# Last block of a three-block model: order of the compression block, of a weight slot's rounding, and of the second branch's gating

## The chip, the core and the metric

One NeuronCore of a Trainium2 chip runs the whole program. The metric is the device time of one execution in microseconds, from its start to its end; the median of several runs counts. Engines are named PE (TensorE), ACT (ScalarE), DVE (VectorE), POOL (GpSimd) and SP (SyncE, which only issues loads and stores here).

## What is computed

Three residual blocks on a sequence of 256 tokens of width 1024, all in float32: two of a first kind, each with a feed-forward part, and a last one, `second_block`, which the change touches. Cut to what matters:

```python
def second_block(x, ...):
    h = rms_norm_2(x, norm_w)
    proj = h @ w_in          # q_a k_a v_a z_a q_b kc vc ksl vsl kwn vwn gate_b z_b gate_m
    o_a = moba_mixer(norm(q_a), norm(k_a), v_a, bias_a)              # 8 heads
    k_cmp = norm(compress(kc, pos_k, w1_k, w2_k))                    # gelu(windows @ w1) @ w2
    v_cmp = compress(vc, pos_v, w1_v, w2_v)
    o_b = nsa_mixer(norm(q_b), k_cmp, v_cmp, norm(ksl), vsl, norm(kwn), vwn, gate_b, bias_b)
    y_a = o_a * silu(z_a)
    y_b = o_b * silu(z_b)
    g_m = sigmoid(gate_m)
    merged = g_m[:, :1024] * (y_a @ w_branch_a) + g_m[:, 1024:] * (y_b @ w_branch_b)
    return x + merged @ w_out
```

## The kernel before

**Weights.** Every weight matrix is cut into slots of at most 128 x 2048 numbers, listed in the order of use (L263 to L284). SP loads slot n into one of four buffers `raw`; the buffer of slot n-4 must be free (L491). For a product in near float32 accuracy, ACT rounds the slot into `whi` (two halves, L1217 and L1218, in `high`), and POOL writes `wlo = raw - whi` (L531, four instructions a slot). There are three buffers of each, so the rounding of a slot waits until the one three before it is used. PE then does three matmuls for each piece (L545 to L547): high by high, low by high, high by low. The activations are kept transposed and split the same way: `T_hi` (ACT, L1249) and `T_lo` (DVE, L1755) make `Th` and `Tl` from what PE has transposed into PSUM (`to_T`, L635). A raw buffer is free when its low half is done. The four slots of the compression's first matrices (`whole`: k0, k1, v0, v1) are used raw, without rounding, by `cmp_hidden` (L1076), and free their buffer when PE has used them.

**Order.** Each engine has one instruction queue, written out by hand. In the last block all four share one scheme, `pairs` (PE at L816, ACT at L1441, DVE at L1946): twelve pairs of attention heads, each with scores on PE (L847), score plus bias on DVE (L1954), exponential on ACT (L1447), a transposition on PE (`turn`), its copy on ACT (`turned`, L1457 and L1458), values on PE (L836) and the write on DVE (`finish`). Into each pair, at the places "x", "a", "m" and "b", other work is hung by a table `keyed`. PE fills the pairs with the weight slots (`slot_tm`): za, ksv and zb in pairs 1 to 3, the gates GA and GB in pairs 4 to 10, YA in pair 11 and in the tail; YB, the merge and the output matrix "fo" come after.

**Around the change.** In pair 1, PE does za0, then `cmp_hidden(0, 0)`, which waits for both windows (DVE, L2204, keys first, then values), since the keys' hidden layer goes to bank 1, where the projection that both windows read lies. In pair 3, ACT does squares and copies of "ksv" (L1636, L1640), its root, the exponentials, and after them rounds zb1. At the end, DVE gates the second branch (L2328) in one go when all pairs are written; `turn_b` (PE, L1140) transposes it ahead of the last k step of slot YA1, and YB0 uses it.

Of the kernel before, what the change touches and what calls it, by code (L numbers as in the profile page):

```python
# [16 lines left out]
ALU = mybir.AluOpType  # L17
# [5 lines left out]
P = 128  # L23
S = 256
NT = S // P
# [122 lines left out]
def build(nc, I, out, known):  # L148
    ctx = ExitStack()
    with ctx:  # L150
# [120 lines left out]
        for part in (lambda: za(0), lambda: hidden("k", 0), lambda: za(1), lambda: hidden("k", 1),  # L271
                     lambda: hidden("v", 0), lambda: sel(0), lambda: hidden("v", 1), lambda: sel(1)):
            part()
# [265 lines left out]
        def _(pe):  # L539
# [526 lines left out]
            def cmp_hidden(a, j):  # L1066

                if j == 0:
                    pe.wait_ge(*read(("kc", 0)))
                    pe.wait_ge(*read(("vc", 0)))  # L1070
                    pe.wait_ge(*at("gb"))
                n = slot_no[("w1" + "kv"[a], j)]
                pe.wait_ge(*at(f"w_raw{n % NRAW}", n))
                for k in range(8):
                    q = 32 * (k % 4)
                    i = mm(PS[q:q + 32, 1 - a, 0:256], XC[a][:, 8 * j + k, :], raw[n % NRAW][:, k * 256:(k + 1) * 256],  # L1076
                           start=j == 0 and k < 4, stop=j == 1 and k >= 4)
                i.then_inc(*done("w_used", n))

            def cmp_fold(a):  # L1080

                pe.wait_ge(*at("c_part", a))
                if a == 0:
                    pe.wait_ge(*read(("zb", 1)))
                for m in range(2):
                    i = mm(PS[:, 1 - a, 256 + 32 * m:256 + 32 * m + 32], part[:, a, m * P:(m + 1) * P], cc("four"),
                           start=True, stop=True)
                i.then_inc(*done("c_ht", a))

            def cmp_keys():  # L1090
                pe.wait_ge(*at("c_hid"))
                pe.wait_ge(*at("load_w2"))
                for m in range(2):
                    i = mm(PS[0:32, 1, 0:DH], hid[:, m, :], w2c[:, 0, m, :], start=m == 0, stop=m == 1)
                i.then_inc(*done("c_k"))
# [44 lines left out]
            def turn_b():  # L1140
                pe.wait_ge(*at("y2b"))
                to_T("y2b", hn[:, :, 512:D], 4, 4)
# [5 lines left out]
            def branch_a1(last_values):  # L1148
                pe.wait_ge(*read((("GB", 1), 1)))
                slot_tm((("YA", 1), 0), 2, 8, True, True, mids={1: last_values, 3: turn_b})  # L1150
# [10 lines left out]
            def gate_z(nm, hf):  # L1161
                if (nm, hf) == ("za", 0):
                    pe.wait_ge(*at("hT", (2, 1)))
                if (nm, hf) == ("zb", 0):
# [8 lines left out]
                     for w in range(2) for h in range(NH)], True,  # L1173
                  keyed({(0, "a"): (keys_in,), (0, "m"): (gates_T,), (0, "b"): (lambda: head_T("qb", 2, 2),),
                         (1, "a"): (lambda: gate_z("za", 0), lambda: cmp_hidden(0, 0)),
# [12 lines left out]
            slot_tm((("YB", 0), 0), 6, 12, True, True, fresh="y2b", f0=0)  # L1188
# [13 lines left out]
        def _(act):  # L1202
# [464 lines left out]
            def cmp_part(a):  # L1667
                act.wait_ge(*at("w_used", slot_no[("w1" + "kv"[a], 1)]))
                act.activation(part[:, a, :], PS[:, 1 - a, 0:256], ACT.Copy).then_inc(*done("c_part", a))

            def cmp_gelu(a):
                act.wait_ge(*at("c_ht", a))
                h = PS[:, 1 - a, 256:320].rearrange("p (m c) -> p m c", m=2)
                if a == 0:
                    act.activation(hid[:, :, :], h, ACT.Gelu_apprx_tanh).then_inc(*done("c_hid"))
                    return
                for m in range(2):
                    i = act.activation(hidr[:, m, :].rearrange("p (g h c) -> p g h c", g=2, h=4),
                                       bc(h[:, m, :].rearrange("p (g c) -> p g c", g=2), 2, 4), ACT.Gelu_apprx_tanh)
                i.then_inc(*done("c_rep"))  # L1680
# [31 lines left out]
            def next_tb(h):  # L1712
# [5 lines left out]
                (1, "b"): (lambda: high(slot_no[("ksv", 0)]), lambda: z_tanh("za", za, 2)),  # L1718
                (2, "a"): (lambda: next_tb(0), lambda: cmp_part(0), lambda: high(slot_no[("ksv", 1)])),
                (2, "b"): (lambda: cmp_part(1), lambda: high(slot_no[("zb", 0)]), lambda: head_squares("ksv", 2)),  # L1720
                (3, "x"): (lambda: head_root("ksv"),),
                (3, "a"): (lambda: next_tb(4), lambda: high(slot_no[("zb", 1)])),
                (3, "b"): (lambda: head_T("ksv", 3, kswT, (qn + 3, qn + 4), 2), lambda: high(slot_no[(("GA", 0), 0)]),
                           lambda: z_tanh("zb", zb, 0)),
                (4, "a"): (lambda: high(slot_no[(("GA", 0), 1)]),),
# [9 lines left out]
            T_hi("y2b", 4, 12, 4, lambda k: None)  # L1735
            after_slot((("YA", 1), 0))
            after_slot((("YB", 0), 0))
# [7 lines left out]
        def _(dve):  # L1745
# [525 lines left out]

            def sigmoid(nm, n, t):

                g = sg[(nm, n)]
                dve.wait_ge(*read(((nm, n), t)))
                lk(ts(g[:, t, :], g[:, t, :], 0.5, 0.5, ALU.mult, ALU.add))
# [19 lines left out]
            def att_write(p, rc, o):  # L2296
# [26 lines left out]
                (10, "a"): (lambda: T_lo("y2a", 4, 8, 0, lambda k: None),),  # L2323
                (11, "a"): (lambda: sigmoid("GB", 1, 0), lambda: sigmoid("GB", 1, 1))}))
            dve.wait_ge(*at("a_o", ("att", 11)))
            dve.wait_ge(*read(("zb", 1)))
            for t in range(NT):
                i = stt3(out=hn[:, t, 512:D], in0=hn[:, t, 512:D], scalar=0.5, in1=zb[:, t, :], op0=ALU.mult, op1=ALU.mult)  # L2328
            i.then_inc(*done("y2b"))
            T_lo("y2b", 4, 12, 4, lambda k: None)  # L2330
# [51 lines left out]
```

## Time and profile before

| | |
|---|---|
| median of three runs | 1010.84 us (1009.25 to 1011.47) |
| the profiled execution | 1008.57 us |
| its span | 1006.7 us |
| PE busy | 966.7 us, 96% |
| POOL busy | 676.6 us, 67% |
| ACT busy | 605.5 us, 60% |
| DVE busy | 471.2 us, 47% |
| granted clock of PE, mean | 0.992 |
| memory read | 175.47 MB, 180 GB/s |

The span is the time between the first and the last instruction; what lies around it is 1.9 us. The attention part of the last block goes from about 814 to 968 us of the span, and the tail to 1006.7. All times in the text are those of the span. In a timeline, a line with [t <-who] says that the engine stood still for t before it, and what ended that.

### The profile page before, as it was taken

How to read it: one execution, taken by the hardware profiler on the slowest of the kernel's cores; microseconds unless marked ns; L12 is line 12 of the kernel's file. 1: busy time of each engine (PE TensorE's matmuls, PEld its weight loads, DVE VectorE, ACT ScalarE, POOL GpSimd, SP SyncE). 2: the span in 40 equal slices, each digit the busy share in tenths (PEclk: the TensorE clock that was granted, in tenths of full speed). 3: DMA queues.
4: the chain of work that ended last, by engine and by line, in shares of the span. 5: the costliest groups of instructions: out<-in, count | busy, mean ns of one | idle time of the engine just before them, and what ended most of it. 6: DMA issues, size and time to landing. Idle time of an engine off the chain costs nothing. (4 is left out here: it accounts for less than half of the span.)

```text
span 1006.7 us, 15876 instructions
## 1 busy us (share of the span) xinstructions
PE 966.7 (96%) x6093; PEld 847.1 (84%) x6093; DVE 471.2 (47%) x990; ACT 605.5 (60%) x1130; POOL 676.6 (67%) x538
## 2 busy tenths in 40 slices
PE   6999998999999999999999899999999999899998
PEld 5888788999999797888877799999987887688777
DVE  4735334453434645776944544444346131233552
ACT  7636656555555676877967664555557464685531
POOL 5977725766666785797778575757777855485664
PEclk9999999999999999999998999999999999999999
DMA  9684424776554556457456356565555537544221
GB/s 334 224 236 150 157 84 147 233 240 196 189 188 168 175 143 201 143 161 245 165 178 219 130 186 210 167 209 168 175 175 199 178 120 269 192 127 166 85 84 42
DMA packets 124952, 177.64 MB, mean 176 GB/s; under 512 B 13185, under 2 KB 86797, under 8 KB 124685
## 3 DMA queue, kind: packets, MB, share of 16 engines
q1 hardware_dynamic: 120701, 168.91, 51.7%
q10 hardware_dynamic: 4176, 7.71, 2.2%
q8 instruction: 48, 0.79, 0.3%
q14 instruction: 27, 0.22, 0.1%
HBM read 175.47 MB, written 5.24 MB: 180 GB/s over the span
## 5 line engine op out<-in xcount | busy, mean ns | idle before, releaser
L531 POOL TENSOR_TENSOR wlo<-raw,whi 128x512 fp32r<-128x512 f32 (+1 forms) x502 | 656.4, 1342 | 301.0 <-ACT whi L1217 285.1
L548 PE MATMUL PS<-Th,whi 128*128 128x256 f32 (+2 forms) x1000 | 285.8, 286 | 3.5 <-DVE Tl L1755 2.8
L549 PE MATMUL PS<-Tl,whi 128*128 128x256 f32 (+2 forms) x1000 | 282.5, 283 | 0.0
L550 PE MATMUL PS<-Th,wlo 128*128 128x256 f32 (+2 forms) x1000 | 282.4, 283 | 0.0
L1217 ACT ACTIVATE whi<-raw 128x1024 fp32r<-128x1024 f32 (+1 forms) x144 | 150.7, 1047 | 161.6 <-PE PS L550 122.5
L1830 DVE SCALAR_TENSOR_TENSOR arena<-PS,cols,arena 128x255 f32<-128x255 f32 (+1 forms) x272 | 118.5, 477 | 192.1 <-ACT arena L1350 165.6
L545 PE MATMUL PS<-whi,Th 128*128 128x512 f32 x480 | 194.2, 405 | 9.7 <-DVE Tl L1804 3.3
L548 PEld LDWEIGHTS PS<-Th,whi 128*128 128x128 f32 (+2 forms) x1000 | 191.3, 191 | 9.9 <-issue 5.9
L549 PEld LDWEIGHTS PS<-Tl,whi 128*128 128x128 f32 (+2 forms) x1000 | 191.4, 191 | 1.7 <-issue 0.7
L550 PEld LDWEIGHTS PS<-Th,wlo 128*128 128x128 f32 (+2 forms) x1000 | 191.2, 191 | 0.1
L547 PE MATMUL PS<-whi,Tl 128*128 128x512 f32 x480 | 188.9, 393 | 0.0
L546 PE MATMUL PS<-wlo,Th 128*128 128x512 f32 x480 | 188.8, 393 | 0.0
L1218 ACT ACTIVATE whi<-raw 128x1024 fp32r<-128x1024 f32 (+1 forms) x144 | 149.5, 1038 | 0.0
L545 PEld LDWEIGHTS PS<-whi,Th 128*128 128x128 f32 x480 | 91.1, 190 | 36.5 <-issue 12.4
L547 PEld LDWEIGHTS PS<-whi,Tl 128*128 128x128 f32 x480 | 91.1, 190 | 19.7
L546 PEld LDWEIGHTS PS<-wlo,Th 128*128 128x128 f32 x480 | 91.1, 190 | 17.8 <-issue 0.5
L545 PE MATMUL PS<-whi,aTh 128*128 128x512 f32 x176 | 69.0, 392 | 0.9 <-POOL wlo L531 0.9
L546 PE MATMUL PS<-wlo,aTh 128*128 128x512 f32 x176 | 68.8, 391 | 0.0
L547 PE MATMUL PS<-whi,aTl 128*128 128x512 f32 x176 | 68.5, 389 | 0.0
L1763 DVE TENSOR_TENSOR wlo<-raw,whi 128x2048 fp32r<-128x2048 f32 x18 | 41.4, 2301 | 13.4 <-ACT whi L1218 13.4
L1350 ACT ACTIVATE arena<-PS,cols 128x256 f32<-128x256 f32 x88 | 44.0, 550 | 0.0
L1359 ACT ACTIVATE aTh<-arena 128x512 fp32r<-128x512 f32 x22 | 13.9, 632 | 45.3 <-DVE arena L1849 45.3
(242 smaller groups left out, 1038.7 us busy)
## 6 DMA issues: line engine op xcount, KB each, us to landing
raw<-in_ffn_w_up_dram SPq DMA_DIRECT2D x44, 1024.0 KB, 5.1
raw<-in_w_in_dram SPq DMA_DIRECT2D x23, 1024.0 KB, 5.2
raw<-in_ffn_w_down_dram SPq DMA_DIRECT2D x22, 1024.0 KB, 4.9
raw<-in_c_w_in_dram SPq DMA_DIRECT2D x16, 1024.0 KB, 5.3
raw<-in_ab_w_in_dram SPq DMA_DIRECT2D x14, 1024.0 KB, 6.6
raw<-in_c_w_out_dram SPq DMA_DIRECT2D x8, 1024.0 KB, 5.1
raw<-in_ab_w_out_dram SPq DMA_DIRECT2D x4, 1024.0 KB, 5.8
raw<-in_c_w_in_dram SPq DMA_DIRECT2D x8, 512.0 KB, 5.3
```

The source lines that it names most:

```text
L531: i = nc.gpsimd.tensor_tensor(lo_of(n)[:, c:e], raw[n % NRAW][:, c:e], hi_of(n)[:, c:e].bitcast(F32), ALU.subtract)
L545: mm(o, ah, wh, start=first, stop=False)
L546: mm(o, ah, wl, start=False, stop=False)
L547: return mm(o, al, wh, start=False, stop=last)
L548: mm(o, wh, ah, start=first, stop=False)
L549: mm(o, wh, al, start=False, stop=False)
L550: return mm(o, wl, ah, start=False, stop=last)
L1217: act.activation(hi_of(n)[:, 0:hf], raw[n % NRAW][:, 0:hf], ACT.Copy).then_inc(*done("w_hi_half", n))
L1218: act.activation(hi_of(n)[:, hf:width], raw[n % NRAW][:, hf:width], ACT.Copy).then_inc(*done("w_hi", n))
L1350: act.activation(fac[i % 2][:, q, :], PS[:, 2 * (i % 2) + q // 2, (q % 2) * S:(q % 2 + 1) * S], ACT.Identity, scale=col(f"fw{l}1", j), bia ...
L1763: tt(lo_of(n)[:, :], raw[n % NRAW][:, :], hi_of(n)[:, :].bitcast(F32), ALU.subtract)\
L1830: return stt3(out=dst[:, a:a + n], in0=src[:, b:b + n], scalar=ws, in1=dst[:, a:a + n], op0=ALU.mult, op1=ALU.add)
```

## The change

In words: (1) the first key block of the compression stands at the head of pair 1, ahead of za0, in the list of slots and on PE; it waits for the key windows and the gate columns alone, the value block for the value windows, and the two hidden layers change banks; ACT rounds ksv0 in the middle of pair 1. (2) ACT rounds slot zb1 in pair 2, ahead of the squares of ksv, and each gate slot behind it takes the place of the one before. (3) DVE gates the second branch in two halves, one after the tenth pair's write, one after the last; PE transposes the first in YA1, the second inside YB0; `T_hi` and `T_lo` follow in two parts.

```diff
@@ -268,7 +268,7 @@
         hidden = lambda nm, j: fm("w1" + nm, I["cmp_w1_" + nm + "_2"][0], 0, k0=8 * j, j=j)
         sel = lambda hf: wide(("ksv", hf), w2, 4 * hf, KV + 256, 4, 512)
         za = lambda hf: wide(("za", hf), w2, 4 * hf, 1536, 4, 512)
-        for part in (lambda: za(0), lambda: hidden("k", 0), lambda: za(1), lambda: hidden("k", 1),
+        for part in (lambda: hidden("k", 0), lambda: za(0), lambda: za(1), lambda: hidden("k", 1),
                      lambda: hidden("v", 0), lambda: sel(0), lambda: hidden("v", 1), lambda: sel(1)):
             part()
         tm("zb", w2, KV + 792)
@@ -1066,14 +1066,13 @@
             def cmp_hidden(a, j):
 
                 if j == 0:
+                    pe.wait_ge(*(read(("vc", 0)) if a else at("gb")))
                     pe.wait_ge(*read(("kc", 0)))
-                    pe.wait_ge(*read(("vc", 0)))
-                    pe.wait_ge(*at("gb"))
                 n = slot_no[("w1" + "kv"[a], j)]
                 pe.wait_ge(*at(f"w_raw{n % NRAW}", n))
                 for k in range(8):
                     q = 32 * (k % 4)
-                    i = mm(PS[q:q + 32, 1 - a, 0:256], XC[a][:, 8 * j + k, :], raw[n % NRAW][:, k * 256:(k + 1) * 256],
+                    i = mm(PS[q:q + 32, a, 0:256], XC[a][:, 8 * j + k, :], raw[n % NRAW][:, k * 256:(k + 1) * 256],
                            start=j == 0 and k < 4, stop=j == 1 and k >= 4)
                 i.then_inc(*done("w_used", n))
 
@@ -1083,12 +1082,13 @@
                 if a == 0:
                     pe.wait_ge(*read(("zb", 1)))
                 for m in range(2):
-                    i = mm(PS[:, 1 - a, 256 + 32 * m:256 + 32 * m + 32], part[:, a, m * P:(m + 1) * P], cc("four"),
+                    i = mm(PS[:, a, 256 + 32 * m:256 + 32 * m + 32], part[:, a, m * P:(m + 1) * P], cc("four"),
                            start=True, stop=True)
                 i.then_inc(*done("c_ht", a))
 
             def cmp_keys():
                 pe.wait_ge(*at("c_hid"))
+                pe.wait_ge(*at("c_rep"))
                 pe.wait_ge(*at("load_w2"))
                 for m in range(2):
                     i = mm(PS[0:32, 1, 0:DH], hid[:, m, :], w2c[:, 0, m, :], start=m == 0, stop=m == 1)
@@ -1137,9 +1137,9 @@
                 pe.wait_ge(*at("y2a"))
                 to_T("y2a", hn, 4, 0)
 
-            def turn_b():
-                pe.wait_ge(*at("y2b"))
-                to_T("y2b", hn[:, :, 512:D], 4, 4)
+            def turn_b(k):
+                pe.wait_ge(*at("y2b", k))
+                to_T("y2b", hn[:, :, 512:D], k + 2, 4, k)
 
             def branch_a0():
                 pe.wait_ge(*at("T_lo", ("y2a", 3)))
@@ -1147,7 +1147,7 @@
 
             def branch_a1(last_values):
                 pe.wait_ge(*read((("GB", 1), 1)))
-                slot_tm((("YA", 1), 0), 2, 8, True, True, mids={1: last_values, 3: turn_b})
+                slot_tm((("YA", 1), 0), 2, 8, True, True, mids={1: last_values, 2: lambda: turn_b(0)})
 
             def keys_in():
                 pe.wait_ge(*read(("va", 1)))
@@ -1172,7 +1172,7 @@
                               lambda c, h=h, w=w: vsw[:, c, w, DH * (h // 4):DH * (h // 4) + DH])
                      for w in range(2) for h in range(NH)], True,
                   keyed({(0, "a"): (keys_in,), (0, "m"): (gates_T,), (0, "b"): (lambda: head_T("qb", 2, 2),),
-                         (1, "a"): (lambda: gate_z("za", 0), lambda: cmp_hidden(0, 0)),
+                         (1, "a"): (lambda: cmp_hidden(0, 0), lambda: gate_z("za", 0)),
                          (1, "b"): (lambda: gate_z("za", 1), lambda: cmp_hidden(0, 1)),
                          (2, "a"): (lambda: cmp_hidden(1, 0), lambda: selected(0)),
                          (2, "b"): (lambda: cmp_hidden(1, 1), lambda: selected(1)),
@@ -1185,7 +1185,8 @@
                          (7, "a"): (G("GB", 0, 0),), (7, "m"): (cmp_turn,),
                          (8, "a"): (G("GB", 0, 1),), (8, "m"): (cmp_out,),
                          (9, "a"): (G("GB", 1, 0), turn_a), (10, "a"): (G("GB", 1, 1),), (11, "a"): (branch_a0,)}), branch_a1)
-            slot_tm((("YB", 0), 0), 6, 12, True, True, fresh="y2b", f0=0)
+            pe.wait_ge(*at("a_o", ("att", 11)))
+            slot_tm((("YB", 0), 0), 6, 12, True, True, fresh="y2b", f0=0, mids={1: lambda: turn_b(2)})
 
             def turn_merged(n):
                 pe.wait_ge(*at("mrg", n))
@@ -1666,11 +1667,11 @@
 
             def cmp_part(a):
                 act.wait_ge(*at("w_used", slot_no[("w1" + "kv"[a], 1)]))
-                act.activation(part[:, a, :], PS[:, 1 - a, 0:256], ACT.Copy).then_inc(*done("c_part", a))
+                act.activation(part[:, a, :], PS[:, a, 0:256], ACT.Copy).then_inc(*done("c_part", a))
 
             def cmp_gelu(a):
                 act.wait_ge(*at("c_ht", a))
-                h = PS[:, 1 - a, 256:320].rearrange("p (m c) -> p m c", m=2)
+                h = PS[:, a, 256:320].rearrange("p (m c) -> p m c", m=2)
                 if a == 0:
                     act.activation(hid[:, :, :], h, ACT.Gelu_apprx_tanh).then_inc(*done("c_hid"))
                     return
@@ -1715,14 +1716,14 @@
 
             pairs("att", 12, True, keyed({
                 (0, "b"): (lambda: head_T("qb", 2, qbT, (qn + 7, qn + 7), 2),),
-                (1, "b"): (lambda: high(slot_no[("ksv", 0)]), lambda: z_tanh("za", za, 2)),
+                (1, "m"): (lambda: high(slot_no[("ksv", 0)]),), (1, "b"): (lambda: z_tanh("za", za, 2),),
                 (2, "a"): (lambda: next_tb(0), lambda: cmp_part(0), lambda: high(slot_no[("ksv", 1)])),
-                (2, "b"): (lambda: cmp_part(1), lambda: high(slot_no[("zb", 0)]), lambda: head_squares("ksv", 2)),
+                (2, "b"): (lambda: cmp_part(1), lambda: high(slot_no[("zb", 0)]), lambda: high(slot_no[("zb", 1)]),
+                           lambda: head_squares("ksv", 2)),
                 (3, "x"): (lambda: head_root("ksv"),),
-                (3, "a"): (lambda: next_tb(4), lambda: high(slot_no[("zb", 1)])),
-                (3, "b"): (lambda: head_T("ksv", 3, kswT, (qn + 3, qn + 4), 2), lambda: high(slot_no[(("GA", 0), 0)]),
+                (3, "a"): (lambda: next_tb(4), lambda: high(slot_no[(("GA", 0), 0)])),
+                (3, "b"): (lambda: head_T("ksv", 3, kswT, (qn + 3, qn + 4), 2), lambda: high(slot_no[(("GA", 0), 1)]),
                            lambda: z_tanh("zb", zb, 0)),
-                (4, "a"): (lambda: high(slot_no[(("GA", 0), 1)]),),
                 (4, "m"): (lambda: cmp_gelu(0), lambda: cmp_gelu(1), U((("GA", 0), 0))),
                 (4, "b"): (lambda: gates("GA", 0), cmp_norm),
                 (5, "a"): (U((("GA", 0), 1)),), (5, "m"): (U((("GA", 1), 0)),), (5, "b"): (cmp_keys,),
@@ -1732,8 +1733,9 @@
                 (9, "m"): (U((("GB", 1), 0)),), (9, "b"): (lambda: T_hi("y2a", 4, 8, 0, lambda k: None),),
                 (10, "m"): (lambda: gates("GB", 1), U((("GB", 1), 1))),
                 (11, "b"): (U((("YA", 0), 0)),)}))
-            T_hi("y2b", 4, 12, 4, lambda k: None)
+            T_hi("y2b", 2, 12, 4, lambda k: None)
             after_slot((("YA", 1), 0))
+            T_hi("y2b", 4, 12, 4, lambda k: None, 2)
             after_slot((("YB", 0), 0))
             T_hi("mrg0", 4, 0, 6, lambda k: None)
             after_slot((("YB", 1), 0))
@@ -2269,6 +2271,13 @@
                     i = stt3(out=hn[:, t, 0:512], in0=hn[:, t, 0:512], scalar=0.5, in1=za[:, t, :], op0=ALU.mult, op1=ALU.mult)
                 i.then_inc(*done("y2a"))
 
+            def gated_b(k):
+                dve.wait_ge(*at("a_o", ("att", 9 + k)))
+                dve.wait_ge(*read(("zb", 1)))
+                a = 512 + k * P
+                stt3(out=hn[:, :, a:a + 2 * P], in0=hn[:, :, a:a + 2 * P], scalar=0.5, in1=zb[:, :, k * P:(k + 2) * P],
+                     op0=ALU.mult, op1=ALU.mult).then_inc(*done("y2b", k))
+
             def sigmoid(nm, n, t):
 
                 g = sg[(nm, n)]
@@ -2320,14 +2329,12 @@
                 (7, "a"): (cmp_probs, lambda: sigmoid("GA", 1, 0), lambda: sigmoid("GA", 1, 1)),
                 (8, "b"): (cmp_out, cmp_add),
                 (9, "a"): (lambda: sigmoid("GB", 0, 0), lambda: sigmoid("GB", 0, 1)),
-                (10, "a"): (lambda: T_lo("y2a", 4, 8, 0, lambda k: None),),
+                (10, "a"): (lambda: T_lo("y2a", 4, 8, 0, lambda k: None),), (10, "b"): (lambda: gated_b(0),),
                 (11, "a"): (lambda: sigmoid("GB", 1, 0), lambda: sigmoid("GB", 1, 1))}))
             dve.wait_ge(*at("a_o", ("att", 11)))
-            dve.wait_ge(*read(("zb", 1)))
-            for t in range(NT):
-                i = stt3(out=hn[:, t, 512:D], in0=hn[:, t, 512:D], scalar=0.5, in1=zb[:, t, :], op0=ALU.mult, op1=ALU.mult)
-            i.then_inc(*done("y2b"))
-            T_lo("y2b", 4, 12, 4, lambda k: None)
+            gated_b(2)
+            T_lo("y2b", 2, 12, 4, lambda k: None)
+            T_lo("y2b", 4, 12, 4, lambda k: None, 2)
             branch_a(0)
             branch_a(1)
             for n in range(2):
```

## Rows read from the trace of the kernel before

**Rows 1.** The page's busy times: engine, busy us, share of the span, instructions.

```profile
PE 966.7 (96%) x6093; PEld 847.1 (84%) x6093; DVE 471.2 (47%) x990; ACT 605.5 (60%) x1130; POOL 676.6 (67%) x538
```

**Rows 2.** Waits, 820 us to the end: who for whom, us, times, longest.

```profile
PE PS L545 <- POOL wlo L531: 3.0, 2, 2.2
PE PS L635 <- DVE hn L2328: 2.2, 1, 2.2
```

**Rows 3.** Chain that ended last, from 800 us: start, us, what.

```profile
830.91 5.23 DMA raw<-in_w_in_dram
...
857.12 1.08 ACT arena L1636 x2
...
863.55 0.96 ACT whi L1217
...
865.80 3.73 POOL wlo L531 x3
```

**Rows 4.** Timeline of PE: start, us, instruction, idle time before and its releaser.

```profile
823.13 0.93 PE L847 MATMUL PS<-arena 64*128 64x128 f32 x8
...
840.53 1.07 PE L1076 MATMUL PS<-raw,arena 128*32 128x256 f32 x16
842.45 0.47 PE L545 MATMUL PS<-whi,Th 128*128 128x512 f32 x1 [0.85 <-POOL wlo L531]
...
850.34 1.07 PE L1076 MATMUL PS<-raw,arena 128*32 128x256 f32 x16
851.34 0.50 PE L545 MATMUL PS<-whi,Th 128*128 128x512 f32 x1
...
869.58 0.50 PE L545 MATMUL PS<-whi,Th 128*128 128x512 f32 x1 [2.17 <-POOL wlo L531]
```

**Rows 5.** PE behind it; two stretches, granted clock third from last.

```profile
870.63 0.63 PE L546 MATMUL PS<-wlo,Th 128*128 128x512 f32 x1
...
874.02 0.39 PE L545 MATMUL PS<-whi,Th 128*128 128x512 f32 x1
874.25 0.39 PE L546 MATMUL PS<-wlo,Th 128*128 128x512 f32 x1
...
872.00:874.00 2.00, 2.00 (x6) 1.55 (x5) 0.00 (x0) 0.00 (x0) 2.00 (x3) 0.50 0.99 383
...
968.00:970.00 2.00, 2.00 (x10) 1.65 (x9) 2.00 (x6) 1.33 (x3) 0.00 (x0) 1.00 1.03 420
```

**Rows 6.** Timeline of DVE, the windows of the compression keys (L2204).

```profile
822.12 1.66 DVE L2204 TENSOR_TENSOR arena<-PS,cols 64x240 f32<-64x240 f32 x4
```

**Rows 7.** Timeline of POOL: the low halves of ksv1 and of zb0.

```profile
845.93 4.99 POOL L531 TENSOR_TENSOR wlo<-raw,whi 128x512 fp32r<-128x512 f32 x4 [3.63 <-ACT whi L1217]
852.88 5.04 POOL L531 TENSOR_TENSOR wlo<-raw,whi 128x512 fp32r<-128x512 f32 x4 [1.97 <-ACT whi L1217]
```

**Rows 8.** Tile raw, 820 to 880 us: its loads, issue to landing.

```profile
DMA to landing us min/median/max: 5.0/5.2/9.3
```

**Rows 9.** Timeline, pair 11: ACT's last exponential, and PE's turning of it.

```profile
954.30 0.21 ACT L1447 ACTIVATION_READ_ACCUMULATOR arena<-arena,st 128x1 f32 x1
...
956.50 0.49 PE L635 MATMUL PS<-cst,arena 128*128 128x128 f32 x3
```

**Rows 10.** Timeline of DVE, PE and ACT around the gating, and L2269 for comparison.

```profile
886.60 1.29 DVE L2269 SCALAR_TENSOR_TENSOR hn<-hn,arena 128x512 f32<-128x512 f32 x2
...
964.01 2.52 DVE L2328 SCALAR_TENSOR_TENSOR hn<-hn,arena 128x512 f32<-128x512 f32 x2
966.58 1.09 PE L635 MATMUL PS<-cst,hn 128*128 128x128 f32 x8 [2.17 <-DVE hn L2328]
967.27 1.21 ACT L1249 ACTIVATE Th<-PS 128x256 fp32r<-128x256 f32 x4 [5.87 <-PE PS L635]
967.96 1.42 DVE L1755 SCALAR_TENSOR_TENSOR Tl<-PS,Th 128x256 fp32r<-128x256 f32 x4 [1.44 <-ACT Th L1249]
969.15 1.06 ACT L1217 ACTIVATE whi<-raw 128x1024 fp32r<-128x1024 f32 x1 [0.67 <-PE PS L547]
```

## Prediction

> **What bounds the kernel now.** I read the page's busy times first: PE is busy 96% of the span [rows 1], so the end moves only where PE stands still, or runs at a lower clock. Next the waits of PE over the last block (820 us to the end), longest first: two waits for a weight slot's low half, which POOL makes, 3.0 us together with the longest 2.2, and one of 2.2 for `hn` from L2328, the gating of the second branch [rows 2]. Then the chain that ended last, which says what stood behind the two POOL waits [rows 3], PE's own order of time around them [rows 4], and the clock behind the longer one [rows 5].
>
> The first wait is slot ("ksv",0): its load was issued at 830.91, when the first compression block had been used, and took 5.23 us; then ACT's rounding and POOL's four subtractions follow, and PE stood 0.85 us [rows 3, 4]. The second is slot ("zb",1): ACT squares the ksv heads from 857.12, goes through root and exponentials, rounds zb1 only at 863.55, POOL ends about 869.5, and PE stood 2.17 us [rows 3, 4]. Right behind it TensorE's granted clock falls to 0.50, its 1.2 GHz level [rows 5]: from 870.63 to 874.02 lie eight matmuls, 0.42 apart, where 0.23 is usual. That is 3.39 us for 1.82, a loss of 1.6 [rows 5]. The third wait stands before `turn_b`: 2.17 us until 966.58 [rows 10].
>
> **The change part by part.** The profiled execution took 1008.57 us, of which the span is 1006.7; the sum is made on that span, and applied to the median of the runs, 1010.84, which lies 2.27 above the profiled time (the runs go from 1009.25 to 1011.47).
>
> *Part 1, compression block first.* No arithmetic is added. `cmp_hidden(0,0)` moves ahead of za0: PE's sixteen small matmuls take 1.00 us wherever they stand [rows 4]. It now starts when the scores of pair 1 end, 823.13 + 0.86 = 823.99. Its new head-of-line wait, on the key windows, would hold za0 and everything after it; the windows' four DVE instructions end at 822.12 + 1.66 = 823.78 [rows 6]. So 0.2 us of slack, cost 0, and each microsecond of lateness would cost one. The value windows, which come 2.3 us later, are no longer waited for there: the bank swap and the move of that wait to the value block are what makes this possible. On SP's queue the value block v0 is now issued at about 825.1 (before, right after za0's low half), then ksv0 and v1 behind it; za0's load takes the slot before. v0 and v1 are used at 840 and later, so both have over 10 us. Loads of the stretch landed 5.0 to 9.3 us after issue [rows 8]; ksv0, issued at about 825.5, lands between 830.5 and 834.8 instead of 836.1. ACT rounds it in the middle of pair 1, ahead of `turned(3)`, whose result PE wants only in pair 2 after ten microseconds: cost 0. With 1.1 us to POOL's start and 5.0 for POOL, the low half is ready by 841.0 even from the late end, and PE would come at 841.5 (840.53 + 1.00, [rows 4]). The 0.85 is gone.
>
> What is late next is ("ksv",1). Its load hangs on the second key block, which PE finishes at the same time as before; POOL is done with it at 845.93 + 4.99 = 850.92 [rows 7], and PE began it at 851.34 [rows 4]. So of the 0.85 only 851.34 - 850.92 = **0.42 us** gets through. The block's lesser order (the load perhaps 0.1 earlier) is about what PE needs after a late low half, and I set them against each other. Bounds: 0.2 to 0.85.
>
> *Part 2, zb1 rounded ahead of the squares.* POOL begins on zb0 at 852.88, some 1.1 us behind ACT [rows 7], so ACT is done with it at about 853.7, and idle until the squares at 857.12 [rows 3]. zb1's two halves take 1.9 us and fit, if its load is there: it is issued when ksv0's low half is done, before 842.3, and lands by 842.3 + 9.3 = 851.6 at worst [rows 8]. Its buffer is free (ksv0 used at 848). POOL then does zb1 right behind zb0, whose end is 852.88 + 5.04 = 857.92 [rows 7], so by 863.0; PE wants it at 867.4. The **2.17 us** go. ACT's place after pair 3's exponentials is taken by GA00 and the next by GA01, the same 1.9 us each, so `turned(6)` is not later than it was; their raw buffers have been loading since 851, and POOL has them one slot (5 us) earlier than before. PE's short wait for `turned(6)` (0.6) stays, since it hangs on the squares, which move with ksv1's 0.42. The clock spell followed the stand-still, and nothing else on PE changes there; I take it as gone: **1.6 us**. Bounds: 0 (the spell comes anyway) and 1.6.
>
> *Part 3, second branch in two halves.* Work on DVE is the same two instructions' worth. `gated_b(0)` stands behind the tenth pair's write, at about 950.7; it delays the last scores by 0.65 to 1.26 us. Behind them come ACT's exponentials, which ended at 954.5 while PE turned them at 956.50 [rows 9]: 2.0 us of cover, cost 0 (without it, up to 1.3). First what the rows show: the two L2328 instructions took 2.52 us, the two of the same form at L2269, where POOL was idle, 1.29 [rows 10]. The Trainium skill, page "SBUF — State Buffer", section "SBUF: two separate sides", says that a DVE instruction with two SBUF inputs and a GpSimd one exclude each other for the whole instruction; the trace agrees. By it each half may also make POOL late by 0.65, on low halves that PE uses 9 us later.
>
> PE now turns the first half after the last values, two steps into YA1, without a wait. The last values' write on DVE ends at 964.0 and `gated_b(2)` at 965.3 (half of 2.52 [rows 10]); YA1 ends at about 964.4 + 0.43 + 1.37 = 966.2. So the new wait for the last write, ahead of YB0, costs 0, and `turn_b(2)`, one k step (six matmuls of 0.228 = 1.37 us) further, finds its half. What is late next is `T_hi` of the second half: on ACT it is queued behind fo0's rounding, which waits for YA1's end. From that end: 0.35 to the rounding's start (969.15 against 966.58 + 0.85 + 1.37 = 968.80), 2.0 for its halves, 0.69 from T_hi to T_lo, 0.4 for T_lo: 3.45 to 3.5 us [rows 10]. PE has 1.37 + 0.43 + 1.37 = 3.17 before it needs it. So 0.3 us of new wait, plus 0.1 for splitting one group of transposes in two. Before, 2.17 were lost. Gain 2.17 - 0.3 - 0.1 = **1.75 us**. Bounds: 1.0 (ACT half a microsecond later, and a short clock spell of its own) and 2.3 (the real gap between matmuls is about 0.2 more than the idle time listed). Afterwards DVE's `branch_a` products end at about 972.3, as YB0 does, and all else of the tail hangs on PE.
>
> The bank swap and `cmp_keys`' new wait for `c_rep` (ready 4 us before) cost nothing.
>
> **Sum:** 0.42 + 2.17 + 1.6 + 1.75 = 5.95 us. Span 1000.75, execution 1002.6, median 1010.84 - 5.95 = **1004.9**.
>
> **Rivals.**
> A. *The clock falls anyway*, there or in another stretch, since pairs' small matmuls also leave PE thin. For: a stand-still of the same length at 964.4 had no spell behind it (granted 1.00 at 968 to 970 [rows 5]), so length alone doesn't decide. Against: the only spell of the last 200 us stands directly behind the longest POOL wait. Gives 1.6 less: 1006.5.
> B. *The tail gives its gain back*: ACT serves fo0 first and DVE's blocked instructions come on top, so YB0 waits as long as `turn_b` did. For: 0.3 us is already in my sum. Against: to eat 1.75 ACT must be that much later, and nothing else is queued there. 1006.7.
> C. *The change doesn't do what it says early on*: the loads of ksv0 and zb1 arrive in the old rhythm, since v0's stands in front of them, and PE meets POOL as before. Then only part 3 counts: 1009.1. Against: the landing times above.
> D. *Slower than before*: ACT, in order, waits for zb1's load ahead of the squares. Squares, root, two table loads, exponentials and `turned(6)` are one unbroken chain [rows 3], so each microsecond that zb1 lands after 857.1 - 1.9 = 855.2 is lost one for one. It eats the whole gain at 855.2 + 5.95 = 861.2, and beyond that the kernel is slower; landing at 864 would give 1013.6. Against: 861.2 is 19 us after the issue, twice the longest landing [rows 8].
>
> **How the numbers follow.** Forecast 0.59, A 0.17, B 0.12, C 0.07, D 0.05. The range takes in the forecast with its bounds (low: gaps truly 0.2 larger each, ksv in full, and a spell less elsewhere, together 2.5: 1002.4), A and B, and reaches to C: 1002.4 to 1009.0. A measurement of this kernel can tell about 0.2% (2 us) from no change. Forecast, A and B are faster by more than that, less the case that several of them meet: 0.84. C and such meetings are within it: 0.11. D: 0.05.
>
> **What would show it.** PE's waits for POOL in 820 to 880 shrink from 3.0 to a short one before ksv1 (about 0.6); zb1's low half is done 4 us before use; granted clock 1.00 in 866 to 876; PE passes pair 4's scores 4.2 us earlier; no wait for L2328's successor; one of about 0.3 us for Tl inside YB0. It would be wrong if PE waits for `kc` ahead of `cmp_hidden`, if ACT idles on a DMA before the squares, or if a clock spell stands elsewhere.

## The result and the profile after

| | before | changed |
|---|---|---|
| first comparison, median of 4 | 1010.05 us (1008.00 to 1011.47) | 1002.12 us (999.50 to 1002.86) |
| ratio with its 95% interval | | 0.9912 (0.9887 to 0.9937) |
| second comparison, median | 1008.42 us (29 runs) | 1002.80 us (11 runs) |
| ratio with its 95% interval | | 0.9953 (0.9935 to 0.9971) |
| all executions, median | 1008.56 us (80) | 1002.75 us (16) |
| span of the profiled execution | 1006.7 us | 1000.3 us |

The ratios are estimates of their own, not the quotients of the two medians. The changed kernel is faster by 0.9% in the first comparison and by 0.5% in the second, larger one. The forecast of 1004.9 us (1002.4 to 1009.0) is missed by 2.8 us, and its range by 0.3. Yet the two spans differ by 6.4 us, against a sum of 5.95, and the medians over all executions by 5.8. Where both come near the sum and the first comparison's median doesn't, the base from which the sum was subtracted is to be looked at. But first the places.

PE's waits of the changed kernel, 820 us to the end (who for whom, us, times, longest). The two of 2.2 in [rows 2] are gone:

```profile
PE PS L635 <- ACT arena L1459: 1.6, 3, 0.8
...
PE PS L545 <- POOL wlo L531: 0.6, 2, 0.4
```

PE's timeline of the changed kernel, for [rows 4] (line numbers from `cmp_hidden` on are lower by one on PE, higher by one on ACT and by two on DVE):

```profile
823.59 0.93 PE L847 MATMUL PS<-arena 64*128 64x128 f32 x8
824.45 1.07 PE L1075 MATMUL PS<-raw,arena 128*32 128x256 f32 x16
...
841.68 0.50 PE L545 MATMUL PS<-whi,Th 128*128 128x512 f32 x1
...
851.10 0.50 PE L545 MATMUL PS<-whi,Th 128*128 128x512 f32 x1 [0.43 <-POOL wlo L531]
...
865.78 0.52 PE L635 MATMUL PS<-cst,arena 128*128 128x128 f32 x3 [0.80 <-ACT arena L1459]
866.14 1.04 PE L635 MATMUL PS<-cst,hn 128*128 128x128 f32 x8
866.93 0.48 PE L545 MATMUL PS<-whi,Th 128*128 128x512 f32 x1
...
872.59 0.93 PE L847 MATMUL PS<-arena 64*128 64x128 f32 x8
```

The scores of pair 1 come 0.46 later than before (823.59 against 823.13): the two executions had already drifted apart upstream, where nothing was changed (the kernel before has these scores at 823.13 in one profile and at 825.79 in another, e12). All places are therefore counted from these scores. The block starts right behind them, ksv0 (841.68) waits for nothing, ksv1 waits 0.43, zb1 (866.93) for nothing.

ACT, POOL and DVE of the changed kernel: zb1's rounding, the squares behind it, POOL's low halves of zb0 and zb1, and the key windows, for [rows 3, 6, 7]:

```profile
852.92 1.05 ACT L1218 ACTIVATE whi<-raw 128x1024 fp32r<-128x1024 f32 x1
...
856.88 1.09 ACT L1637 ACTIVATE arena<-PS 128x512 f32<-128x512 f32 x2 [1.97 <-PE PS L547]
```

```profile
852.15 10.04 POOL L531 TENSOR_TENSOR wlo<-raw,whi 128x512 fp32r<-128x512 f32 x8 [1.10 <-ACT whi L1218]
```

```profile
822.58 1.66 DVE L2206 TENSOR_TENSOR arena<-PS,cols 64x240 f32<-64x240 f32 x4
```

zb1 is rounded four microseconds before its squares are ready to start, and ACT still idles 1.97 ahead of them; POOL makes zb0 and zb1 in one go and is done at 862.19, 4.7 before use.

The granted clock (third from last) where [rows 5] had 0.50:

```profile
868.00:870.00 2.00, 2.00 (x10) 1.64 (x9) 0.00 (x0) 1.94 (x3) 2.00 (x3) 1.00 0.03 8
870.00:872.00 2.00, 2.00 (x10) 1.68 (x9) 0.00 (x0) 0.00 (x0) 2.00 (x3) 1.00 0.74 186
```

The tail of the changed kernel, for [rows 10]: the first four transposes, the second half's gating on DVE, the start of YA1's last k step, the other four transposes, DVE's low half of the second part, and the third k step of YB0:

```profile
958.55 0.60 PE L635 MATMUL PS<-cst,hn 128*128 128x128 f32 x4
...
959.75 0.78 DVE L2278 SCALAR_TENSOR_TENSOR hn<-hn,arena 128x512 f32<-128x512 f32 x1
...
960.37 0.39 PE L545 MATMUL PS<-whi,Th 128*128 128x512 f32 x1
...
963.10 0.60 PE L635 MATMUL PS<-cst,hn 128*128 128x128 f32 x4
...
964.57 0.76 DVE L1757 SCALAR_TENSOR_TENSOR Tl<-PS,Th 128x256 fp32r<-128x256 f32 x2 [3.38 <-ACT Th L1250]
965.05 0.50 PE L545 MATMUL PS<-whi,Th 128*128 128x512 f32 x1
```

The gating ends 2.6 us before its transposes. From there to YB0's third step it is 1.95 us. The first four transposes and the k step behind them took 1.82 (958.55 to 960.37), so the new wait is about 0.15.

### The profile page after: what moved, and what is told of

It is laid out like the page before. It is cut to its first block and busy times, and to the rows that moved or that the text cites. A ratio compares the mean times of both kernels' runs of the same rounds, so it can differ in the third digit from the quotient of the medians.

```text
span 1000.3 us, 15875 instructions
## 1 busy us (share of the span) xinstructions
PE 965.8 (97%) x6093; PEld 847.5 (85%) x6093; DVE 471.4 (47%) x990; ACT 605.4 (61%) x1130; POOL 676.6 (68%) x538
```

## The experiments

Each profile is read at the same places, counted from the scores of pair 1 (in us): the scores of pair 2 (behind all of pair 1), of pair 3 (behind ksv1), of pair 4 (behind zb1), and then the stretch from the scores of pair 11 to the transposes of the first merged half. Spells are stretches at the clock's lower level (granted 0.50) in the last block, given by their place in us and, in brackets, by the full-rate time that they cost. The labels e1 to e12 are the experiments below. Falls of the clock behind PE's last matmul are left out, since they hold nothing up.

| kernel | pair 2 | pair 3 | pair 4 | pair 11 to merged | spells |
|---|---|---|---|---|---|
| before | 16.54 | 33.88 | 53.70 | 28.37 | 870 (1.7) |
| before, e12 | 16.53 | 33.95 | 53.60 | 28.39 | 870 (1.7) |
| changed | 16.24 | 33.18 | 49.00 | 26.24 | none |
| changed, e5 | 16.23 | 33.26 | 49.07 | 26.29 | none |
| changed, e10 | 16.24 | 33.16 | 48.98 | 26.28 | 908 (1.7) |
| e1, zb1 alone | 16.53 | 34.22 | 50.02 | 30.02 | 908 (3.4), 966 (1.7) |
| e11, zb1 alone | 16.52 | 33.80 | 49.59 | 28.40 | none |
| e2, block alone | 16.24 | 33.21 | 53.05 | 28.38 | 868 (1.7) |
| e3, tail alone | 16.52 | 33.72 | 53.48 | 26.28 | 868 (1.7) |
| e4, gap filled, too long | 16.52 | 33.73 | 53.84 | 28.40 | none |
| e6, gap filled | 16.55 | 33.70 | 51.95 | 28.39 | 912 (1.7) |
| e7, windows late | 18.54 | 35.61 | 51.43 | 26.28 | 910 (1.7) |
| e8, three waits less | 16.46 | 33.14 | 48.41 | 26.13 | 906 (1.7) |
| e9, two waits less | 16.24 | 33.53 | 48.65 | 26.14 | 908 (1.7) |

e1's 30.02 holds its spell at 966.

A second measure takes the clock out. For 75 executions of the kernel before both the span and the mean granted clock are known. A straight line through them says: a span of 1000.5 us at clock 1, and 0.75 us for each 0.001 less; single executions lie 1.1 us about it. "At equal clock" below is how far a kernel's executions lie below that line on average, with twice the standard error of that mean.

**e1: zb1 ahead of the squares, alone**

```diff
-                (2, "b"): (lambda: cmp_part(1), lambda: high(slot_no[("zb", 0)]), lambda: head_squares("ksv", 2)),
+                (2, "b"): (lambda: cmp_part(1), lambda: high(slot_no[("zb", 0)]), lambda: high(slot_no[("zb", 1)]),
+                           lambda: head_squares("ksv", 2)),
-                (3, "a"): (lambda: next_tb(4), lambda: high(slot_no[("zb", 1)])),
+                (3, "a"): (lambda: next_tb(4), lambda: high(slot_no[(("GA", 0), 0)])),
```

(and GA's second slot in pair 3 in place of the first)

> The kernel before, with slot zb1 rounded in pair 2 ahead of the squares, and nothing else of the change. Theory 1 (the stand-still before zb1 and the clock spell behind it are one thing): PE no longer waits for POOL before zb1, granted clock 1.00 from 860 to 880, PE's scores of pair 4 come 4.0 us earlier than before (2.4 for the gap between matmuls, 1.6 for the spell), the wait before ksv0 (0.85) stays; the time falls by 4.0. Rival 1 (the spell belongs to pair 3's thin matmuls, not to the wait): scores of pair 4 only 2.4 us earlier, clock below 1.00 between 866 and 880; the time falls by 2.4. Rival 2 (POOL or the load takes over): less than 1 us.

Measured: median 1004.38 against 1008.52, ratio 0.9953 (0.9933 to 0.9974), so 4.1 us less; at equal clock 2.6 +- 0.7. No wait before zb1, pair 4 earlier by 3.7 and 4.1 us in the two profiles. All this is Theory 1. But in e1's profile the clock fell later, in the stretch where PE does the compression scores (32 matmuls of 16 columns):

```profile
906.00:908.00 2.00, 2.00 (x32) 1.93 (x32) 0.77 (x3) 1.87 (x5) 0.00 (x0) 1.00 0.52 92
908.00:910.00 2.00, 2.00 (x19) 1.64 (x19) 1.22 (x6) 2.00 (x4) 1.32 (x2) 0.60 1.04 407
910.00:912.00 2.00, 2.00 (x10) 1.20 (x7) 1.12 (x8) 0.29 (x2) 2.00 (x2) 0.50 0.11 34
```

The profiled execution had a span of 1008.0, longer than before's 1006.7, though its waits are shorter. So a stand-still and a spell are two things: the first is gone in both profiles of this kernel, while the second came elsewhere in one and not at all in the other (e11).

**e2: the compression block, alone** (the slots' order, banks, waits and ksv0's rounding of the diff)

> The kernel before, with the first compression block at the head of pair 1, the banks swapped and ksv0 rounded in the middle of pair 1; zb1 and the tail as before. Theory: the wait before ksv0 (0.85) goes, one of about 0.4 before ksv1 takes its place, and the chain of squares, root, exponentials and zb1's rounding moves with PE's end of ksv1, so the wait before zb1 stays as long as it was and the clock spell too: 0.7 us earlier at ksv1's end and at zb1, time 0.7 less. Rival (the block is worth what its wait was): 0.95 to 1.1 us.

Measured: median 1006.97, ratio 0.9979 (0.9962 to 0.9997); at equal clock 0.8 +- 0.5. Pair 2 is 0.3 earlier, pair 3 and pair 4 0.67 and 0.65; the wait before zb1 and the spell stand. The theory holds: of the 0.92 that PE lost before ksv0, 0.37 gets past ksv1. The other 0.3 is gained in pair 1. Before, za0 started 0.99 behind the scores, where 0.86 is usual, since ACT's copies of qb ended at 824.07 and za0 started at 824.12; now the block stands in that place, which gives 0.13. The other 0.17 lies in small gaps around the place where the block stood.

**e3: the tail, alone** (`gated_b`, `turn_b`, the two parts of T_hi and T_lo of the diff)

> The kernel before, with the second branch gated, turned and rounded in two halves, and nothing else of the change. Theory: PE's wait of 2.17 before the transposes goes (2.3 between matmuls), about 0.2 comes back before the third k step of YB0; from the scores of pair 11 to the transposes of the first merged half 2.1 us less, time 2.1 less. Rival (only the part that the idle time names counts, and ACT's order eats more): 1.75 or less.

Measured: median 1006.37, 2.15 less; ratio 0.9984 (0.9958 to 1.0009), which one execution of 1019 us widens and which by itself shows no more than that it isn't much slower; at equal clock 1.5 +- 1.4. The trace is sharper: 28.37 becomes 26.28, the same 2.1 as in the changed kernel. The three parts together are 0.65 + 2.4 + 2.1 = 5.15 us of waits, and the changed kernel has that: 4.65 by pair 4, less the spell's 1.6, plus 2.1. They add up, and at the end nothing is given back.

**e4 and e6: the gap filled.** The wait before zb1 stays and PE works in it (the line is cut at its right end):

```diff
-                         (3, "b"): (lambda: head_T("ksv", 3, 2), lambda: gate_z("zb", 1),
+                         (3, "b"): (lambda: head_T("ksv", 3, 2), lambda: warm(4, 5), lambda: gate_z("zb", 1),
```

> The kernel before, with five idle matmuls (128x512, float32, result unused) on PE between the transposes of the ksv heads and zb1; they take 0.44 us each, 2.2 in all, so they fill the wait for zb1's low half and don't lengthen it by more than 0.2. Nothing waits less than before. Theory 1 (the stand-still brings the clock spell): granted clock 1.00 from 866 to 880, zb1 starts at the same place as before within 0.2 and ends 1.6 us earlier, time 1.4 to 1.6 less. Rival (the spell comes from pair 3's small matmuls or falls there by chance): spell as before, time the same or 0.2 more.

Measured: median 1011.23, ratio 1.0025 (1.0002 to 1.0049). The filler was too long: five calls ran as ten passes, 0.43 us apart. PE's timeline of e4, the filler and zb1's start:

```profile
869.62 4.46 PE L647 MATMUL PS<-cst 128*128 128x512 f32 x10
...
873.52 0.80 PE L545 MATMUL PS<-whi,Th 128*128 128x512 f32 x1
```

The spell was gone at its place (granted clock 1.00 from 864 to 882), and the overlong filler used that up: pair 4 comes at 53.84, against 53.70. As to time e4 decides nothing, and the 2.7 us that it was slower are not explained by this stretch. e6 has `warm(4, 2)`:

> As e4, but with two idle matmuls in place of five: in e4 each ran as two passes of 0.45 us, so five took 4.5 us and outlasted the wait by 1.25. Two take 1.8 us and fit in it. Theory 1 (the stand-still brings the spell): clock 1.00 from 866 to 880, zb1 starts as before, its end and pair 4's scores 1.6 us earlier than before, time 1.6 less. Rival: spell as before, no gain. A second rival (idle matmuls cost clock elsewhere, e4 was 2.7 slower where its own stretch says 0): time the same or more, with the spell moved to a later stretch.

Measured: median 1008.48 against 1008.42, ratio 1.0002 (0.9978 to 1.0025). Its clock at the old place and at the new one:

```profile
872.00:874.00 2.00, 2.00 (x9) 1.66 (x10) 0.00 (x0) 0.47 (x1) 2.00 (x2) 1.00 0.49 72
...
914.00:916.00 2.00, 2.00 (x9) 1.16 (x8) 1.31 (x8) 0.38 (x2) 2.00 (x3) 0.50 0.29 106
```

Pair 4 is 1.75 earlier than before, as Theory 1 says: the stand-still brings the spell, not pair 3's thin matmuls. But the spell came 40 us later, behind the 16-column matmuls, and at pair 11's scores only 0.3 was left of the gain (126.66 against 126.94 from the scores of pair 1). The second rival is right about the time.

**e5: the changed kernel once more**

> The changed kernel once more, with more runs. In the first profiles the two kernels differ by 6.9 us from the scores of pair 1 to the end (0.7 at ksv1's end, 2.4 before zb1, 1.6 for the clock spell, 2.1 in the tail), while the medians of four runs differed by 7.9 and their ratio by 8.9. Theory 1 (all of the effect lies in these four places, and the rest was spread of few runs, whose granted clock goes from 0.986 to 0.998): the medians differ by 6.0 to 7.5, and at equal granted clock by the three waits alone, 5.2. Rival (something outside the last block got faster too, as the raw buffers' places changed): 8 to 9 us, and more than 6 at equal granted clock.

Measured: 5.6 us between the medians, just below what Theory 1 gave; at equal clock 5.4 +- 0.5, which agrees with the 5.15 of waits (the first four executions: 5.4 +- 0.8). The rival is not borne out: from pair 4 to pair 11, where PE's order is unchanged, the two kernels take the same (73.24 and 73.16), and the scores of pair 1 come no earlier (823.26 to 824.14 in three profiles). The surplus of the first comparison came from both sides: the four executions of the changed kernel had a mean clock of 0.9938, where the larger set has 0.9919 and the kernel before 0.9913, and the four of the kernel before had a median 1.5 above that of all its executions.

**e7: the key windows 2.3 us later**

```diff
-                for a in range(2):
+                for a in (1, 0):
                     windows(a, 1)
```

> The changed kernel, with the compression windows made for the values first and for the keys second on DVE, so that the keys' windows are ready 2.35 us later. Theory (the block at the head of pair 1 holds all of PE when its operand is late, with 0.04 us of slack left in the changed kernel): PE waits for DVE about 2.2 us before the key block; ksv1 then comes late by what its own wait of 0.4 doesn't absorb, so pair 2 to the end come 1.8 to 2.2 later than in the changed kernel. Rival (later waits absorb it): under 1 us.

Measured: median 1006.10, and 3.0 us more than the changed kernel at equal clock. The wait in PE's list and timeline of e7, and DVE's keys' windows that end it:

```profile
PE PS L1075 <- issue: 2.2, 1, 2.2
```

```profile
824.38 1.66 DVE L2206 TENSOR_TENSOR arena<-PS,cols 64x240 f32<-64x240 f32 x4
...
826.14 1.07 PE L1075 MATMUL PS<-raw,arena 128*32 128x256 f32 x16 [2.18 <-issue]
```

The view calls it "issue", since DVE's work ended 0.1 before; the timeline shows what it was. Pairs 2, 3 and 4 are late by 2.3, 2.4 and 2.4, more than the 1.8 to 2.2 expected: nothing is absorbed, not even ksv1's 0.43 (it waits 0.55 here), because ksv1's load hangs on a key block which comes late as well. The windows were 2.36 us later than in the changed kernel, counted from the scores of pair 1, and the block started 2.25 later. So the changed kernel runs with about 0.1 us of slack at this wait (the expectation has 0.04), and lateness costs one for one.

**e8 and e9: what is still in it**

Three waits are taken away: (a) the second key block ahead of za1, (b) GA00's rounding behind the copy turned(6), (c) the second part of `T_hi` ahead of fo0's rounding. The cut shows the slots of (a), (b) and (c); (a) also moves the block ahead of za1 on PE, and ACT's rounding of za1 into pair 0.

```diff
-        for part in (lambda: hidden("k", 0), lambda: za(0), lambda: za(1), lambda: hidden("k", 1),
+        for part in (lambda: hidden("k", 0), lambda: za(0), lambda: hidden("k", 1), lambda: za(1),
...
-                (3, "a"): (lambda: next_tb(4), lambda: high(slot_no[(("GA", 0), 0)])),
+                (3, "a"): (lambda: next_tb(4),), (3, "m"): (lambda: high(slot_no[(("GA", 0), 0)]),),
...
             T_hi("y2b", 2, 12, 4, lambda k: None)
+            T_hi("y2b", 4, 12, 4, lambda k: None, 2)
             after_slot((("YA", 1), 0))
-            T_hi("y2b", 4, 12, 4, lambda k: None, 2)
```

> The changed kernel with its three remaining waits taken away. (a) The second key block ahead of za1 (slots, PE; ACT rounds za1 in pair 0 after the exponentials), so that ksv1's load starts 5.6 us earlier: the wait of 0.43 goes. (b) ACT rounds GA00 in pair 3 after the copy turned(6), not ahead of it: PE's wait of 0.80 goes (0.9 between matmuls). (c) The second part of T_hi ahead of fo0's rounding: 0.2 in YB0. Theory (each wait is worth its length, and nothing is close behind): 1.5 us less than the changed kernel, 0.4 at ksv1, 0.9 more at zb1, 0.2 in the tail. Rival (what is late next takes it back: POOL at zb0 and GA10, where PE already waited 0.15): 0.5 or less.

Measured: median 1000.52, ratio to the kernel before 0.9923 (0.9898 to 0.9948). Against the changed kernel: pair 4 0.6 earlier, tail 0.13, at equal clock 6.0 +- 0.2 against 5.4 +- 0.5. Neither the 1.5 of the theory nor the rival's 0.5. (a) gave 0.1 in all. It took away the 0.43 before ksv1, but the scores of pair 2 come 0.2 later, since the block starts 0.45 behind the transposes where za1 started 0.28 behind them, and then PE, with za1 just behind it, comes to ksv0 while DVE is still at za:

```profile
842.13 0.50 PE L545 MATMUL PS<-whi,Th 128*128 128x512 f32 x1 [0.15 <-DVE arena L2302]
```

(b) gave 0.5, (c) 0.15. e9 has (b) and (c) alone:

> The changed kernel with (b) and (c) of e8 alone: GA00 rounded after the copy turned(6), and the second part of T_hi ahead of fo0's rounding. In e8, (a) took the 0.43 before ksv1 away and paid 0.3 of it back before ksv0. Theory ((b) is most of e8's gain): pair 4's scores 0.5 us earlier than in the changed kernel, tail 0.1 to 0.2 less, time about 0.6 less at equal granted clock, as good as e8 within 0.2. Rival ((a) was worth more than its stretch shows): 0.3 less or nothing.

Measured: median 1001.51, ratio 0.9926 (0.9902 to 0.9950), at equal clock 6.7 +- 0.3 on six executions. In its profile ksv1 waited longer than in the other ones, 0.79, and pair 4 still came 0.35 earlier than in the changed kernel:

```profile
852.72 0.50 PE L545 MATMUL PS<-whi,Th 128*128 128x512 f32 x1 [0.79 <-POOL wlo L531]
```

Both have lower medians than either kernel (e9 by 1.3, e8 by 2.3 us against e5). At equal clock e9's lead over e5 is outside the errors and e8's (0.6) is at their edge, while by the places e8 is 0.2 to 0.3 ahead of e9; which of the two is the better one can't be told from these runs.

**e10, e11, e12: the same kernels, another execution**

> A third profile of the changed kernel. Theory (with the wait before zb1 gone no spell stands in 866 to 876; whether one of 1.7 us stands at 906 to 918 instead is chance of the execution, not of the code): the waits are the same as in the first two, nothing at 866 to 876, and perhaps a spell at 906 to 918, where the first two have none. Rival (the place of the spells belongs to the code): again none in the last block ahead of the output matrix.

> A second profile of e1, which in its first had spells at 908 (3.4 us) and 966 (1.7). Theory (chance of the execution): none at 866 to 876, and another pattern behind. Rival (the code's): the same two places and sizes.

> A second profile of the kernel before. Theory (the wait of 2.17 brings the spell each time): a spell of 1.7 us in 868 to 874 again, and none at 906 to 918. Rival (chance there too): none, or elsewhere.

e12, the kernel before, has its spell again behind the 2.17 us stand-still:

```profile
872.00:874.00 2.00, 1.69 (x4) 1.41 (x5) 0.00 (x0) 0.90 (x1) 2.00 (x3) 0.50 0.33 41
```

e10 has none there and one at 908, where the changed kernel's other two profiles have none; e11 has neither of e1's two. All three theories hold, each on one profile. Over all profiles: with the stand-still in place a spell at 868 to 876 in 4 of 4 (before, e12, e2, e3) and none at 906 to 918; without it, or with it filled, none at 868 to 876 in 10 of 10, and one at 906 to 918 in 6 of 10 (e1, e6, e7, e8, e9, e10). In the changed kernel itself it was 1 of 3. What brings the spell there is not shown: each of the six begins within a microsecond of the end of the 32 matmuls of 16 columns, but the same 32 stand in the other eight profiles, which have none there.

## Why the prediction missed

*The base.* This is the step that failed most. The sum, 5.95, was subtracted from 1010.84, the median of three executions. The kernel before has a median of 1008.56 over 80 executions, which go from 1002.9 to 1014.5: each spell costs 1.7 or 3.4 us, and the mean clock goes from 0.984 to 0.998. From 1008.56 the same sum gives 1002.6, and the changed kernel's median over all sixteen is 1002.75. Of the miss of 2.8 us, 2.3 is this base, 0.6 is that the first four executions of the changed kernel lay below its median over all, and the sum's own error of 0.15 goes the other way. The prediction noted that the median lay 2.27 above the profiled execution and went on with the larger one; the range had no term at all for a base of three executions.

*The terms.* All four places are where the prediction had them, and e1, e2 and e3 show them one by one. All four terms were mis-sized, and that their errors nearly cancel on average is luck:

| term | forecast | measured |
|---|---|---|
| block and ksv0 | 0.42 | 0.65 (e2, and table) |
| stand-still before zb1 | 2.17 | 2.4 |
| clock spell | 1.6 | 1.6 at its place, about 0.6 on average |
| tail | 1.75 | 2.1 (e3, and table) |
| sum | 5.95 (its terms give 5.94) | 6.75 where no other spell comes, about 5.8 on average |

The two stand-stills were each 0.2 longer than the idle time that the view lists: it counts from the modelled end of the last matmul (964.41 in the tail), while the next one could have started one spacing of 0.23 after that one's start (964.02 + 0.23 = 964.25). That was named among the bounds and not taken. The block's 0.3 in pair 1 was not seen at all; its parts are too short for the list of waits, and the largest shows only as the 0.99 between the scores and za0. The new waits came where the sum had them: 0.43 before ksv1, which is what the sum left there (among the signs the prediction gave about 0.6), and 0.15 in YB0, against 0.3. In YB0, ACT was quicker than reckoned.

*Rival A*, that the clock falls anyway, had 0.17. e6 and the ten profiles say about 0.6, which is rough, since they are of seven kernels. Its reason was half right: the spell behind the stand-still belongs to the stand-still, in 4 of 4. What was wrong was to take the spell's loss as won. The sum should have had 1.6 times the chance that none comes later (1.6 x 0.4 = 0.64). The mean clocks agree: 0.9923 over the sixteen executions of the changed kernel against 0.9913 is worth about 0.7 us by the line above. A's "another stretch" was open to a look: the 32 matmuls of 16 columns of pair 6 stand in the trace of before.

*Rival B* (the tail gives it back) is out by e3, *rival C* (loads in the old rhythm) by the changed kernel's ksv0 and zb1; ksv0's load landed at 835.1, 9.1 us after its issue behind v0's, just past the late end that the prediction allowed (834.8), and ksv0 still made no wait. *Rival D* didn't come up: zb1 was there at 852.9, and ACT idled 1.97 us before the squares. The mechanism of D, an engine's head waiting for all behind it, is real, as e7 shows for PE, at one for one.

*What the cover was worth.* The first half's gating took 0.69 at 946.4, with POOL idle, and moved nothing. The second half had been put at 1.26, half of the 2.52 that the two L2328 instructions took; it took 0.78. The 2.52 were not two equal parts: the first instruction took 0.85 (from 964.01) and the second 1.74 (from 964.78), and POOL's instruction that started between them took 1.71 where 1.29 is usual. In the changed kernel the 0.78 began 0.24 before one POOL instruction was due to end, and the next of POOL's took 1.74. The Trainium skill, page "SBUF — State Buffer", section "SBUF: two separate sides", says that of a VectorE instruction with two SBUF inputs and a GpSimd instruction that reads SBUF, the one that starts first has the shared ports for its whole instruction and the other is blocked. The rows agree in kind, though not to the tenth: the 0.78 is 0.09 above the 0.69, with 0.24 of POOL's instruction left. So the price of such a meeting depends on where in the other's instruction it falls, and half of a pair's time is no price for one.

## What to carry to other kernels

When the clock of an engine falls for a few microseconds at a time, give the base of a forecast its own spread, and compare executions at equal mean clock: here the executions of one kernel spread over 11.5 us, but lie 1.1 us about the line, so that ten or twelve of them told 0.3 to 0.7 us, and 1.4 where single ones lay far off (e3, e4). Count a removed stand-still in full, from start to start of the matmuls, and a removed clock spell only by the chance that no other takes its place. And where a block is moved to the head of a queue, ask what its operand's slack is (here about 0.1 us) and what it covers there that was waited for before.

## What the runs showed of the hardware

- Spells at 1.2 GHz (granted clock 0.50) came in two sizes: they cost 1.7 or 3.4 us of full-rate time. The fourteen profiles have them at three to six places ahead of PE's last matmul. One stood behind every unfilled 2.2 us stand-still of pair 3, but only one in seven behind the equally long one of the tail: the 966 of e1, against none in the kernel before, e2, e4, e6, e11 and e12.
- Filling the stand-still with work whose result nobody uses removed the spell there and brought no time: it came 40 us later (e6).
- A float32 matmul of 128x512 without the rounded type ran as two passes 0.43 us apart, against one of 0.23 for the rounded type (e4, and e6 alike).
- DVE and POOL lengthened each other where both worked from SBUF: in the kernel before two equal gatings on DVE took 0.85 and 1.74, and the POOL instruction between them 1.71, where 0.69 and 1.29 were measured apart.
- That e4 as a whole was 2.7 us slower, with its own stretch 0.1 apart, stays open; e6, the same with a shorter filler, was not. e9's surplus over what its stretches show (6.7 at equal clock against about 5.65) stays open too, on six executions.
